# A hybrid decoder step on one core: keys cut to the causal part, routing in two parts, and another order at the end

## The reference, cut to what matters

```python
# one input projection, split into a convolution branch, attention with an indexer, memory attention, gates
sc  = relu(qi @ ki.T / 8) weighted and summed over 8 index heads; -inf where key > query   # 256 x 256
idx = top_k(sc, 64);  valid = idx <= query                     # per prompt query
attn = softmax(q @ k[idx].T / 8) @ v[idx]                       # 8 heads of 64
m = g0*(conv @ w_br_conv) + g1*(attn @ w_br_attn) + g2*(mem @ w_br_mem)
h = layernorm(ALPHA * x + m @ w_o)
lg = h @ w_group + b_group;  le = h @ w_expert + b_expert       # 4 groups of 8 experts
gate = top-1 group, its top-2 experts, with softmax weights
for e in range(32):                                             # w_up 1024 x 512, w_down 256 x 1024
    hu = h @ w_up[e];  y += gate[:, e:e+1] * ((silu(hu[:, :256]) * hu[:, 256:]) @ w_down[e])
out = layernorm(ALPHA * h + y)
```

## Time and profile before

| | |
|---|---|
| median of 3 runs | 649.41 us (646.72 to 653.57) |
| profiled execution | 652.55 us, span 650.7 us |
| mean granted TensorE clock | 0.943 |
| PE busy | 572.0 us, 88% |
| DVE busy | 272.9 us, 42% |
| ACT busy, POOL busy | 103.9 us, 64.2 us |
| moved by DMA | 163.53 MB, mean 251 GB/s |
| chain that ended last | PE 66%, DVE 15%, DMA 14% |

### The profile page before, as it was taken

How to read it: one execution, slowest core, us unless ns; L and a number is a source line. 1 busy time by engine, 2 the same in 40 slices (tenths; PEclk the granted TensorE clock), 3 DMA queues, 4 the chain that set the end, 5 groups by cost and what they waited for, 6 DMA issues and landing times.

```text
span 650.7 us, 8635 instructions
## 1 busy us (share of the span) xinstructions
PE 572.0 (88%) x3514; PEld 361.0 (55%) x3514; DVE 272.9 (42%) x732; ACT 103.9 (16%) x244; POOL 64.2 (10%) x71
## 2 busy tenths in 40 slices
PE   6999999989999889599899996999999868778481
PEld 4556666565887657477576554776564424422130
DVE  1264675565865758546454476211001100100007
ACT  1001111113200143234300211011010101000010
POOL 0000000000200144257500000000000000000000
PEclk9999999989999999699999997999999979798797
DMA  8973044663542556323859536699999999999941
GB/s 303 373 251 97 32 146 149 228 217 107 162 122 76 157 182 183 110 98 101 315 198 413 169 160 266 217 422 404 422 367 418 423 419 420 420 419 422 420 179 68
DMA packets 47134, 163.53 MB, mean 251 GB/s; under 512 B 5842, under 2 KB 22700, under 8 KB 34420
## 3 DMA queue, kind: packets, MB, share of 16 engines
q1 hardware_dynamic: 38272, 138.78, 55.3%
q0 software_dynamic: 3472, 14.31, 6.4%
q10 hardware_dynamic: 5348, 9.86, 4.2%
HBM read 160.14 MB, written 2.77 MB: 250 GB/s over the span
## 4 chain that ended last, share of the span: by engine, by line
PE 66%; DVE 15%; DMA 14%; issue 3%; ACT 1%; SPq 1%; DVEq 0%; ACTq 0%
DMA ring<-in_w_up 14%; PE bank L501 11%; PE bank L686 11%; PE bank L964 6%; PE bank L463 4%; PE bank L805 4%; PE bank L951 4%; PE bank L933 4%; PE bank L1031 3%; PE bank L999 2%; PE bank L873 2%; PE bank L854 2%; PE bank L542 2%; PE bank L512 2%; PE bank L782 2%
## 5 line engine op out<-in xcount | busy, mean ns | idle before, releaser
L686 PE MATMUL bank<-work,ring 128*128 128x264 f32 x384 | 97.7, 405 | 1.6 <-issue 1.6
L501 PE MATMUL bank<-ring,work 128*128 128x512 f32 (+2 forms) x224 | 92.1, 551 | 0.4 <-DVE work L1465 0.4
L964 PE MATMUL bank<-ring,work 128*32 128x512 f32 x384 | 67.8, 679 | 18.1 <-DMA ring<-in_w_up 12.4
L686 PEld LDWEIGHTS bank<-work,ring 128*128 128x128 f32 x384 | 73.1, 198 | 18.2 <-issue 6.6
L501 PEld LDWEIGHTS bank<-ring,work 128*128 128x128 f32 x224 | 40.6, 193 | 32.0 <-issue 28.4
L964 PEld LDWEIGHTS bank<-ring,work 128*32 128x32 f32 x384 | 18.6, 123 | 50.7 <-issue 50.5
L2069 DVE SCALAR_TENSOR_TENSOR work<-work,bank 128x256 f32<-128x256 f32 x8 | 3.4, 421 | 101.0 <-ACT work L1323 101.0
L964 PE MATMUL bank<-proj,work 128*32 128x512 f32 x128 | 34.8, 694 | 11.6 <-DMA ring<-in_w_up 11.6
L951 PE MATMUL bank<-gates 128*128 128x256 f32 x144 | 36.6, 411 | 0.0
L951 PEld LDWEIGHTS bank<-gates 128*128 128x128 f32 x144 | 34.8, 335 | 0.5 <-issue 0.4
L2082 DVE COPY gates<-bank 128x512 f32<-128x512 f32 x8 | 5.5, 692 | 66.3 <-PE bank L1031 66.3
(11 more groups left out here) (306 smaller groups left out, 759.4 us busy)
## 6 DMA issues: line engine op xcount, KB each, us to landing
ring<-in_w_up SPq DMA_DIRECT2D x24, 2048.0 KB, 18.8
ring<-in_w_down SPq DMA_DIRECT2D x12, 2048.0 KB, 27.3
ring<-in_w_in SPq DMA_DIRECT2D x22, 1024.0 KB, 6.0
proj<-in_w_up SPq DMA_DIRECT2D x8, 2048.0 KB, 23.6
proj<-in_w_down SPq DMA_DIRECT2D x4, 2048.0 KB, 27.6
ring<-in_w_o SPq DMA_DIRECT2D x4, 1024.0 KB, 17.3
ring<-in_cache_mem_k ACTq DMA_DIRECT2D x1, 2048.0 KB, 8.1
ring<-in_cache_mem_v ACTq DMA_DIRECT2D x1, 2048.0 KB, 13.1
```

The costliest lines, as they stand in the source:

```text
L501: last = mm(bank[2 * (i % 2 if i < MEMC else 0) + t][:, 0:w], lhs[:, k, 128 * t:128 * t + 128], rhs[:, k % 4, :], start=(k == 0), stop=(k ...
L686: last = mm(b[:, 0:TOK], w[:, k, 128 * (n % 2):128 * (n % 2) + 128], xT[:, k, 0:TOK], start=(k == 0), stop=(k == KT - 1))
L964: last = mm(bank[5][32 * j:32 * j + 32, :], xTe[q // 2 % 2][:, k, s0:s0 + CAP], w2[j // 2][:, j % 2, r, :], start=(k == 0), stop=(k == KT ...
```

## The change

It does seven things.

1. For prompt tile 0 only keys 0 to 127 are worked on: scores, top 64, softmax, transposes and values. `mbias` shrinks to 384 columns. The index scores go in six steps (four heads of 128 keys, twice; two heads of 256 keys, four times).
2. The eight rounds of tile 0 stand between the index steps; the tables leave eight rounds for the memory heads.
3. The maxima of the two tiles are two instructions instead of one.
4. Routing: tiles 0 and 2 are routed and gathered before tile 1's norm; tile 1 follows (`route`, `places`, `first_slots`, `first_part`). `residual_in` is taken apart and stands, but for tile 1, in the routing. The constants `alpha_id` and `fourth` are made earlier.
5. In the last two fours the tile part of `combine(q - 1)` stands between the two `up_half`.
6. The last two down units are not two experts each, but one half of the rows of w_down of all four experts; `down(7)` does the first half as soon as its unit is there. `combine(7)` begins with the left half of the columns.
7. Last norm: tile 1 is scaled and shifted by ACT from PSUM, multiplied and added by POOL; DVE keeps tile 0 and the samples. ACT starts the samples' output DMAs.

```diff
-TOPK_ROUNDS = ((0, 2, 6), (6, 8, 11), (11, 16, 16))
+INDEX_ROUNDS = ((0, 0), (0, 0), (0, 3), (3, 5), (5, 7), (7, 8))
+TOPK_ROUNDS = ((8, 9, 11), (11, 12, 14), (14, 16, 16))
+INDEX_STEPS = ((0, (0, 2, 4, 6)), (0, (1, 3, 5, 7)), (1, (0, 2)), (1, (1, 3)), (1, (4, 6)), (1, (5, 7)))
+def keys_of(t, n):
+    return (0, 256) if t == 0 and n < NMH else (0, 128) if t == 0 else (256, 256) if n < NMH else (128, 256)
...
+            def last_down(w, f):
+                d = wslot[w].rearrange("p (j n) -> p j n", j=4)
+                s = w_dn[NE - 4:NE, :, :].rearrange("j (p r) n -> p j r n", p=128)
+                sp.dma_start(d, s[:, :, f, :]).then_inc(quad_in[w], 16)
...
             for n in range(2, QUADS):
-                up(q)
+                up_half(q, 0)
+                if early:
+                    combine_tiles(q - 1)
+                up_half(q, 1)
...
-                combine(q - 1)
+                if early:
+                    combine_samples(q - 1)
+                else:
+                    combine(q - 1)
                 down(q)
-            combine(QUADS - 1)
+            combine_last(QUADS - 1)
...
+            act.wait_ge(n1_ready, 1)
+            for dh in range(2):
+                act.activation(y3[:, 1, 512 * dh:512 * dh + 512], bank[2 + dh][:, :], ACT.Identity,
+                               bias=stats[:, 54:55], scale=stats[:, 41:42]).then_inc(n1_done, 1)
...
+                pool.wait_ge(n1_done, dh + 1)
+                pool.tensor_tensor(y3[:, 1, cs], y3[:, 1, cs], ln2g[:, cs], ALU.mult).then_inc(pchain, 1)
+                pool.wait_ge(pchain, dh + 1)
+                pool.tensor_tensor(y3[:, 1, cs], y3[:, 1, cs], ln2b[:, cs], ALU.add).then_inc(y1_ready, 1)
...
-            y_rstd(1, 5)
-            y_scale(1)
```

More of the change, by code:

```diff
@@ L907, in _ @@
             pe.wait_ge(ht_sb, 4)
[L908 removed]
+            logits(1, bank[5][:, 0:36], 0, 4)
+            pe.wait_ge(aid_ready, 1)
+            pe.wait_ge(h_ready, 2)
+            residual_samples()
             pe.wait_ge(ht_sb, 5)
[L910 to L914 removed]
@@ L2019, in _ @@
             tt(e8, les, b3(m1, 8), ALU.subtract, e_ready)
[L2020 to L2032 removed]
+            first_slots(1, ALL3, 3)
             dve.wait_ge(exp_ready, 1)
```

423 lines of the change are left out of this document (253 added, 170 removed).

## The result

The changed kernel takes **630.92 us** (median of four, 630.22 to 634.58) against 651.49 us (646.72 to 656.0) of the kernel before on the same chip: ratio 0.9697, 95% interval 0.9612 to 0.9781. The forecast was 628 us, 619 to 636. The profiled execution took 631.18 us with a span of 629.4; the sum of the prediction gave a span of 650.7 - 21.5 = 629.2. So the size is right, within the scatter. The experiments show that this is partly luck: most of the largest term has another cause than the one given, the routing gave some 2 us more and the last loads with the end of down 1.6 us less than forecast, and in the last norm two errors cancel.

The account below looks back on a forecast made before the run. Bound by the way to the first read up unit, 40 units of DMA and a tail. -11.1 - 2.8 - 1.7 - 1.8 + 0.2 - 4.3 + 0 = -21.5 off the median 649.4 gave 628 us, range 619 to 636.

Parts of the forecast that it names:

- What bounds the kernel: Three parts in a row: way to the first read up unit, 40 units of DMA (199 us), tail of 25.3 us.
- The stall in the heads: Attention heads: values(2) waits for head_out(0) behind the top-64 rounds; moving eight cuts the 17.37 us step to 6.26, -11.1 us.
- Smaller heads: Eight attention heads: turn, values and scores lose a quarter, 0.7 us a head; bounds 0 and -5.6, taken as -2.8 us.
- The rival that the heads stay VectorE's: DVE's loop sets the heads' step, smaller heads give nothing, head_out(0) still some 2 us late: 634 us, chance 0.13.
- taking the middle: Smaller heads set at -2.8, between 0 and -5.6, since only every second step has the head_out that makes DVE late.
- Routing: Before the first up unit: TensorE busy instead of waiting 4.84 us for the mask, -1.7 us; bounds +1 and -4.
- Inside the stream: Expert weight stream: residual in four passes instead of eight, -1.8 us; last two units in 4 KB rows, +0.2 us.
- the dip: In the second four, DMA at 269 GB/s in 470 to 475 us, 1.8 us of nothing from slots freed late.
- From the last bytes to the end of down: Tail: early combine(6), and only half of down(7), 1.75 us, after the last landing; -4.3 us, bounds -3.4 and -4.5.
- The new norm: Last norm, end of down(7) to span end: +19.0 against 18.95 before, so 0; bounds -3.7 and +1.
- the sum without exclusion: Last norm with y_scale and POOL not blocking each other: end at +15.2, -3.7 us; as a rival 624 us, chance 0.27.
- The exclusion: Last norm: DVE's y_scale and POOL's four instructions exclude each other, so the samples' DMAs end at +19.0.

Follow-up runs that it names:

- old end: Changed kernel with late combinations, the last down unit whole in 8 KB rows and the last norm on DVE alone; 633.95 us, ratio 0.9743.
- last down whole: Changed kernel with the last two down units read as before, two experts each in 8 KB rows, down(7) started when both are there; 632.38 us, ratio 0.9773.
- late combinations: Changed kernel with the combinations of the last two fours back at their old place behind the mid turn; 636.09 us, ratio 0.9759.
- fillers: Changed kernel with twelve extra matmuls that nobody reads between the halves of down(7); 628.37 us, ratio 0.9666. Also in a combined kernel, 624.67 us, ratio 0.9632.
- centred in PSUM: Changed kernel with VectorE's centred values of the first tile and the samples left in their PSUM banks; 629.24 us, ratio 0.9668.

## Why the prediction came out

1. **What bounds the kernel**: right. Three parts in a row; the heads' gain passed unchanged.
2. **The stall in the heads, -11.1**: the step went from 17.37 to 6.05, but its cause was given wrongly. I priced the moved rounds at nothing in the index phase because softmax(0) stayed at 238.1. It did (237.06, and everything was 0.9 earlier at the index cast), but without the rounds it would have come 2.8 us earlier. I compared with the kernel before, not with the change without this step. The place of the rounds gave 2.3 us by the next turn, of which the time shows nothing; the rest of the heads' change, above all the narrower work of tile 0, gave some 9 us. That the two together came to 11 is luck as far as the given cause goes.
3. **Smaller heads, -2.8**: -2.45 over the five regular steps measured. The rival that the heads stay VectorE's is out, and so is the reason for taking the middle: no wait for VectorE stands in these steps. TensorE's three pieces shrank by 0.11, 0.22 and 0.21 us, 0.54 a step and not 0.7, and fewer than eight steps are regular.
4. **Routing, -1.7**: -3.8, at the bound of -4. From the last logits to the first up unit TensorE took 14.3 us, not the 15.9 of the sum, since four small counting groups took 0.3 to 0.75 us; and the logits came 1.3 us later behind w_o, not 1.8.
5. **Inside the stream, -1.8 and +0.2**: the dip is gone and gives 2.15 us with the old end. The last loads of the changed kernel end unevenly:

```profile
605.00:606.00 1.00, 1.00 (x12) 0.26 (x8) 0.00 (x0) 0.00 (x0) 0.00 (x0) 1.00 0.84 336
606.00:607.00 1.00, 0.63 (x8) 0.00 (x0) 0.00 (x0) 0.00 (x0) 0.00 (x0) 1.00 0.54 217
607.00:608.00 1.00, 0.00 (x0) 0.00 (x0) 0.00 (x0) 0.00 (x0) 0.00 (x0) 1.00 0.25 90
```

(Columns as in the earlier trace rows.) That this comes from the rows of 4 KB is not shown: with the last down whole, in rows of 8 KB, the last four us moved 369, 246, 74 and 8 GB/s. The last bytes land at 608, 204 us after the first freed slot, against some 205 before, 203 with the old end, and 203 to 206 in the other profiles of the split. The net is -1, not -1.6, and a price of the 4 KB rows is not shown.
6. **From the last bytes to the end of down, -4.3**: about 2.6 us pass now and 6 before, so -3.3. The second half starts 0.7 us after the last bytes, which the sum left out. (The sum also counted the +0.2 of part 5 twice, once in the 627.4.) Parts 5 and 6 together are 4.3 us instead of 5.9. The split and the early combination were priced as one, which is how they pay: the early combination without the split costs 2.35.
7. **The new norm, 0**: 18.8 against 18.95, by two errors. POOL starts 8.7 us after down, not 7.3, and the end comes 4.2 us behind POOL, not the 3.15 that the earlier trace rows showed behind a DMA's issue; that is 2.4 us more than the sum without exclusion has (12.5 + 3.15 = 15.65 by its own terms, where it says 15.2). The exclusion is real, but on the path it costs 0.8 us and not 3.7: it falls on DVE, and the end is POOL's. The rule of the Trainium skill (SBUF — State Buffer, Who interferes with whom) on two SBUF inputs agrees with y_scale's 1.43 us each with two SBUF sources and 0.77 with one. On its blocking: each of y_scale's two (1.20 and 1.64 us) ended 0.55 us behind the end of a POOL instruction (620.55 and 622.21), as if held until then; POOL's second and third, begun while DVE's ran, took 0.33 and 0.45 us longer, not DVE's whole length.

The sum for the spans, -21.3 measured and -21.5 forecast: -16.85 (-15.6 forecast) up to the slot, -4.3 (-5.9), -0.15 (0). That the first of these is one execution against one, in a column that scatters by 9 us for the same code, makes the closeness of the sums luck too. The median lies 2.9 above 628: 2.1 of it because the kernel before had a median of 651.49 beside the changed one, not 649.4, and 0.9 because the gain in the medians is 20.6 us, not 21.5.

**Left open.** At the values of the last head but one the wait differs between profiles of the same code up to there: 3.19 us in the changed kernel, 3.03 with late combinations, 0.35 in three later ones, then 3.08, 1.65 and 1.69. The chip doesn't decide it, since 0.35 and 3.08 come from the same one. PE, DVE and ACT stand still together, the profile names a remote releaser for DVE, and the DMAs run at their full 400 GB/s from about 300 us on. That the engines' own instructions come late through these DMAs would fit; it wasn't tried, and the DMAs run as full in a profile with 0.35 us (397 to 418 GB/s).

## What to carry to other kernels

Price a moved step against the kernel that has every other part of the change and not the move: the wait that it causes may be one that the other parts had just removed. Work that is put into an idle engine's gaps should be counted into them gap by gap (0.76, 1.00 and 2.03 us held five rounds, not eight). Before freeing an engine at the end, find the instruction that the end follows at a fixed distance: here it was GpSimd's last, 4.2 us before the end, and what was gained on VectorE alone was free of effect. Take parts of a change apart in both directions: the early combination costs 2.35 us without the split.

## What was not expected of the hardware

- The second half of down(7), in the kernels without fillers behind an idle of 2.0 to 2.1 us, took 1.92 us in two profiles and 2.9 to 3.6 in five. In the two the idle before up_half(7,1), ten us earlier, had been 0.33 and 0.29 us, in the five 1.00 to 1.17. Behind fillers it took 1.90 both times.
- Behind an idle of 3.73 us ahead of down(7) TensorE worked at half speed for all of the next 6.5 us (granted clock 0.50).
- A fill by GpSimd (0.52 us) did not lengthen VectorE's instructions with two SBUF sources; its products and sums did (1.54 to 2.86 us for two).
- The span ended 4.2 us behind GpSimd's last instruction, though the last DMA's data had been moved 2.3 us before the end (centred in PSUM).
